# A hybrid decoder step on one core: five pairs of the convolution's gate products, instead of three, stand in front of the turn of the sample's lists

## What is computed

```python
a_glu, b_glu, q, k, v, qi, ki, wi, g_c, g_a = jnp.split(h @ w_in, IN_SPLITS, axis=-1)
glu = a_glu * jax.nn.sigmoid(b_glu)
c = jax.nn.silu(layer_norm(causal_depthwise_conv(buf, conv_w, conv_b), lnc_g, lnc_b))
conv_branch = c @ w_conv_out
o = attend_fn(q, k, v, qi, ki, wi)
attn_branch = o.reshape(B, T, ATT_W) @ w_attn_out
gc = jax.nn.sigmoid(g_c + b_gate[:D_MODEL])
ga = jax.nn.sigmoid(g_a + b_gate[D_MODEL:])
mix = (gc * conv_branch + ga * attn_branch) @ w_o
```

## Time and profile before

| | us |
|---|---|
| median of 3 runs (range) | 1352.9 (1352.4 to 1355.35) |
| profiled execution, its own time | 1347.98 |
| its span, first to last instruction | 1346.0 |
| PE busy | 1206.7 (90%) |
| DVE busy | 764.9 (57%) |
| POOL busy | 570.2 (42%) |
| ACT busy | 411.4 (31%) |

### The profile page before, as it was taken

One profiled execution on the slowest core, in us unless ns is written; L12 is line 12 of the kernel. 1 busy time (PEld: TensorE's weight loads), 2 busy tenths in 40 slices (PEclk: granted clock), 3 DMA queues, 4 the chain that ended last, 5 costly groups with the idle time before them and its releaser, 6 DMA issues.

```text
span 1346.0 us, 18797 instructions
## 1 busy us (share of the span) xinstructions
PE 1206.7 (90%) x7242; PEld 744.4 (55%) x7242; DVE 764.9 (57%) x1414; ACT 411.4 (31%) x852; POOL 570.2 (42%) x518
## 2 busy tenths in 40 slices
PE   5899999896798867788999899999998989999986
PEld 4435777685454533345666468877754545554432
DVE  1659999999888886887563134352522212221216
ACT  3630144543355465762222112231111111111110
POOL 5000096978775765757765000000233333443320
PEclk9999999998799978878999999998999999999998
DMA  9502222213565664757987320382299999999935
GB/s 329 193 28 67 63 82 76 81 52 98 148 174 167 185 191 133 252 168 250 328 266 267 133 99 32 102 323 76 84 418 413 409 395 364 366 415 416 403 113 206
DMA packets 92840, 281.46 MB, mean 209 GB/s; under 512 B 17960, under 2 KB 50552, under 8 KB 81800
## 3 DMA queue, kind: packets, MB, share of 16 engines
q1 hardware_dynamic: 54672, 165.64, 32.8%
q0 software_dynamic: 35520, 111.22, 24.7%
q10 hardware_dynamic: 2559, 3.40, 0.8%
HBM read 300.94 MB, written 23.11 MB: 241 GB/s over the span
## 4 chain that ended last, share of the span: by engine, by line
PE 49%; DVE 27%; DMA 11%; POOL 5%; issue 4%; ACT 4%; POOLq 0%; DVEq 0%; ACTq 0%; SPq 0%
PE ps L1526 9%; DVE arena L1962 6%; DVE arena L1961 5%; DVE arena L1963 5%; PE ps L1140 5%; PE ps L1550 5%; PE ps L1146 5%; POOL arena L1046 5%; PE ps L1370 4%; PE ps L1362 3%; DMA arena<-in_w_dn,arena 3%; PE ps L1228 2%; DMA arena<-scr_x,arena 2%; PE ps L1180 2%; DMA arena<-in_cache_kv,arena 2%
## 5 line engine op out<-in xcount | busy, mean ns | idle before, releaser
L1046 POOL DMA_INDIRECT arena<-in_cache_kv,arena x256 | 264.8, 1034 | 127.0 <-issue 73.7
L1140 PE MATMUL ps<-arena 128*128 128x288 f32 (+2 forms) x1120 | 294.8, 424 | 1.1 <-ACT arena L1694 1.1
L1140 PEld LDWEIGHTS ps<-arena 128*128 128x128 f32 (+1 forms) x1120 | 209.1, 189 | 84.4 <-issue 29.2
L1526 PE MATMUL ps<-arena 128*64 128x256 f32 x1568 | 189.7, 384 | 5.2 <-DMA arena<-in_w_gu 2.6
L1526 PEld LDWEIGHTS ps<-arena 128*64 128x64 f32 x1568 | 109.1, 138 | 83.8 <-issue 28.1
L1096 POOL DMA_INDIRECT scr_ypair<-arena x49 | 50.5, 1030 | 186.8 <-ACT arena L1896 168.1
L1089 POOL DMA_INDIRECT arena<-scr_x,arena x49 | 50.0, 1020 | 173.6 <-DVE arena L2343 159.0
L1617 ACT ACTIVATE arena<-ps 128x256 f32<-128x256 f32 (+5 forms) x138 | 57.9, 429 | 205.3 <-PE ps L1362 63.6
L1025 POOL TENSOR_TENSOR arena<-arena 128x816 f32<-128x816 f32 x58 | 103.0, 1775 | 17.5 <-ACT arena L1635 10.7
L1146 PE MATMUL ps<-arena 128*128 128x256 f32 (+4 forms) x544 | 107.0, 360 | 0.9 <-ACT arena L1839 0.6
L1550 PE MATMUL ps<-arena 128*64 128x512 f32 x392 | 98.9, 627 | 9.7 <-DMA arena<-in_w_dn,arena 9.7
(11 more groups left out here) (350 smaller groups left out, 1701.5 us busy)
## 6 DMA issues: line engine op xcount, KB each, us to landing
arena<-in_w_gu SPq DMA_DIRECT2D x32, 2048.0 KB, 12.5
arena<-in_w_dn SPq DMA_DIRECT2D x32, 1024.0 KB, 14.9
arena<-in_w_in SPq DMA_DIRECT2D x20, 1024.0 KB, 5.6
arena<-scr_q SPq DMA_DIRECT2D x32, 256.0 KB, 5.1
arena<-in_cache_kv,arena POOLq DMA_INDIRECT x256, 4.0
arena<-in_w_o SPq DMA_DIRECT2D x4, 1024.0 KB, 5.2
arena<-in_w_pg SPq DMA_DIRECT2D x4, 1024.0 KB, 9.2
arena<-scr_ypair SPq DMA_DIRECT2D x4, 1024.0 KB, 8.0
```

The source lines that it names most:

```text
L1046: pl.indirect_dma_start(unit_rows[:, 2 * j + t, half * H * HD:(half + 1) * H * HD], None, I["cache_kv"].rearrange("n (h d) -> (n h) d", h= ...
L1140: mm = nc.tensor.matmul(out, w[:, k], hT[:, k, a:b], start=(k == 0), stop=(k == KC - 1))
L1526: mm = nc.tensor.matmul(PS[2 + p % 2][64 * half:64 * half + 64, 0:2 * P], xT[:, p % 3, j, 64 * h:64 * h + 64], w[:, k, half, :], start=(k ...
```

## The change

`schedule()` puts `GATES[:5]` instead of `GATES[:3]` in front of `("offs",)`, and `branch_jobs()` gives the planner of the attention `GATES[5:]` instead of `GATES[3:]`.

```diff
 def branch_jobs():
-    jobs = [job for gate in GATES[3:] for job in gate] + [("cv", 0), ("croot", 0)]
+    jobs = [job for gate in GATES[5:] for job in gate] + [("cv", 0), ("croot", 0)]
...
     jobs += [("vS", 0)]
-    jobs += [job for gate in GATES[:3] for job in gate]
+    jobs += [job for gate in GATES[:5] for job in gate]
     jobs += [("offs",)]
     jobs += ATTENTION
```

## The result

The changed kernel takes **1380.9 us** in the median of four runs (1377.08 to 1386.38), the kernel before 1352.65 in the same measurement (1351.79 to 1355.35): a ratio of 1.0208, 95% interval 1.0164 to 1.0253. It is slower by 28 us, between 1.6% and 2.5% by the interval. I had forecast slower, by 13, with 1379 as the upper end.

The account below looks back on a forecast made before the run. DVE's key selection bounds the kernel up to the lists, gathers pace groups 1 to 7, PE is full from about group 10. Late lists +9.9 and attention +3 gave +13 on 1352.9: 1366 us, range 1351 to 1379.

Parts of the forecast that it names:

- Term 1, the late lists: Before the attention: convolution products behind later gates delay GpSimd's last add, the key lists and `offs`; +9.9 us, bounds +8.5 to +12.
- The first two groups: Attention, `offs` to PV 1: gates, turns and the prompt's heads delay QK 0 and PV 1, hence gathers; +12 us.
- Groups 2 to 7: Attention, PV 1 to PV 7: four gates gone, gathers still set the pace, 0 to 13 us come back; took -7.
- Groups 8 to 11: Attention, PV 7 to PV 11: more convolution-branch work stands earlier, only gathers bound it; between 0 and -14 us, took -9.
- The end: Attention after PV 11: no gates cover the chain from QK 15 to PV 15; +7 us, bounds +5 to +8.
- my sign: Attention's end: a stretch of 5 us or more without PE between QK 15 and PV 15 would show the forecast right.
- The sum: Whole attention, `offs` to `abP 0 0`: 12 - 7 - 9 + 7 = +3 us, bounds -10 and +20.
- The rival with the clock: Middle of the attention: TensorE's clock falls where gates are thinned, +14 us on top of +13; 1380 us, chance 0.11.
- The rival that PE was the bound: Attention: lists late by 9.9 us, but PE's 15.7 us of removed work shortens it; -6, 1347 us, chance 0.08.
- Given back: Attention, groups 2 to 11: faster groups make up the lists' delay of 9.9 us; 1353 us, chance 0.09.
- the free fill: PE's wait before `offs`: lists on time, 15.7 us of PE work falls out of the attention; 1337 us, chance 0.05.

Follow-up runs that it names:

- Front: The run with both undone, plus the six remaining gate jobs packed into the attention's first group; 1360.0 us, ratio 1.0081 to the kernel before (fast-gathering chip).
- norms: The run with both undone, plus the convolution's norm jobs packed into groups 4 to 6 (last in 7); 1359.8 us, ratio 1.0054 (fast-gathering chip).
- tail: The run with both undone, plus groups 14 and 15 in the new plan's order; 1360.5 us, ratio 1.0070 to the kernel before (fast-gathering chip).
- the run with both undone: Changed kernel with products spread as before and attention in the old order less the four moved gate jobs; 1353.7 us, ratio 1.0015 (fast-gathering chip).

## Why the prediction was wrong

**Term 1, the late lists: right.** +9.9 forecast, 9.4 to 9.5 measured. Its points came: the wait at L1296 was 12.31 (12 to 13), L1296 started at 354.41 (353), ACT's last product at 342.54 (341), L1030 ended at 345.04 (343.4) with L1004 at once after it. The 1.3 to 1.6 by which these came late are about the 1.8 that arose ahead of L1153.

**The first two groups: right in mechanism, too large.** +12 forecast, +7.5 in the first trace. QK 0 was read well (it ended 26.9 behind `offs`, I had said 29), and so were PV 0 (47.1; 45.5) and QK 1 (53.4; 53.8). PV 1 came at 70.7, not 73 to 77: what lies between QK 1 and PV 1, mostly the 17 heads, took 17.3 us and not 21.2.

**Groups 2 to 7: the step that failed.** I wrote that "0 to 13 come back" and took -7; it was +8.1. The bound was made from GpSimd's pace and two turns, as if the gathers set it alone, and it could only give a gain. *Front* shows that taking gates away gives nothing back here (149.3 us with five gate jobs in it, 149.4 in *front* without; five, not the four that I counted), so the right value for the removal was 0. The loss came from what I had left out: the planner moved the whole branch and the prompt with it. With the order undone the groups are back at 149.3 to 151.2 us, from 158.2 to 160.7, which shows the order as the cause. For the part of it, the norms of the convolution, packed into these groups, lengthen them by 15 us alone, and the changed kernel's trace has 7.2 us of waiting for them; how much of the +8.1 is theirs stays open. I had counted the jobs of PE in the two lists and not followed who waits on ACT and DVE.

**Groups 8 to 11: right**, -6.8 against -9; it is the other side of the same shift, as *norms* shows (+15.3, -12.2).

**The end:** +9.5 against +7 in the first trace, and outside my bounds of +5 to +8. The missing cover is 5.5 of it (*tail*: 100.5 against 95.0). The rest came with other parts of the new order and isn't separated. Of my sign, 5 us without PE between QK 15 and PV 15, only part came: 3.8 us of waiting in three pieces, the longest 1.73. PV 15 itself then ran in part at half speed.

**The sum.** The attention came out 15.3 us above my +3, and the groups 2 to 7 alone are 15.1 of it. That the other three terms look harmless in the sum is luck: they are off by -4.5, +2.2 and +2.5.

**The rival with the clock** named 1380, which is nearly the time measured, for a reason that is refuted. The granted clock did fall in the middle, from 0.89 to 0.79. The Trainium skill (TensorE: Matmul & The Clock Gate, section Part 1: The HAM clock gate) says that the array is throttled by default and that activity releases it, and the trace agrees. But I had priced the fall as if PE were the bound of those groups.

**The rival that PE was the bound** did not come either, but I had argued against it with the wrong row: the 38.57 of 50 us are of a stretch (530 to 580) in which no gate stood. In the first two groups, with five gates, PE was busy for 60.1 of 63.1 us. What refutes it is the run with both undone, in which these groups are as long without four of the gates. **Given back** did not come, and **the free fill** is answered by the run with both undone: even with the lists on time and the old order the fill gains next to nothing (ratios 1.0015, 0.9958 and 0.9994 in three measurements; only the second, on a slow-gathering chip, is clear of 1 by its interval), since its four gates were hidden in the attention as well.

So a third of the loss is the products, which I had (9.4 us); two thirds are a re-planned order, of which I had forecast a sixth (+3 of +18.3).

## What to carry to other kernels

Filling a wait pays only if the work comes out of a stretch in which its engine is the bound: look up both places, not just the idle one. A busy share doesn't tell this: PE was busy for 95% of the groups that the work came out of, and they were no shorter without it. When an edit makes a planner or a spread run anew, it is several changes at once; fix the rest of the order and strike the moved jobs from it, then each part can be timed by itself. A planner's own sum is worth what its costs are: worked out with the kernels' own `merged()`, it is 430.1 for the order before, with its four jobs more, and 428.5 for the new one, while on the chip the new order takes some 20 us more than the old one less the same four jobs.

## Not expected

**The chips differ by 9% on this kernel, in one stage.** The kernel before takes 1353 us on some and 1473 to 1482 on others, steadily. The run with both undone, on a slow-gathering chip, windows from PV 11 to PV 15 and from there to the end:

```profile
749.00:885.00 136.00, 112.37 (x620) 66.89 (x618) 42.28 (x52) 22.21 (x38) 54.42 (x56) 0.86 0.51 170
885.00:1477.00 592.00, 550.19 (x3305) 332.05 (x3301) 184.30 (x485) 91.11 (x211) 137.59 (x133) 0.97 0.69 270
```

The end of the attention takes 136 us instead of the 95 of the row shown above, at 170 GB/s instead of 257; all that follows takes 592 us on both chips. GpSimd waits 163.7 us for PV there, and on the fast chip 51.4, while issuing a gather takes the same 946 ns. So it isn't the issue that is slow, and not the transfers behind the attention. That it is the landing of the gathers of keys and values is my reading and not shown: on the fast chip they land 4.1 us after issue in the median, and the traces of the slow-gathering chips have no landing times for them. On such a chip the attention is 513 to 537 us long in each of the ten runs there, and what still counts is when the gathers start (the late lists cost 16.6 us there). Why those chips gather more slowly no run here tells.

**A lower clock at no price.** In *front* it is 0.79 instead of 0.90 over 149 us, with five gate jobs fewer, and the stretch is as long to 0.2 us. It is another matter where nothing else is waited for: at the end of the changed kernel the last ten matmuls of PV 15 took 3.58 us at a granted clock of 0.50, and before all sixteen took 1.90.
